# Two-layer hybrid decoder step on one core: where VectorE takes the turned rows in the last four pairs of products

## The chip, the core and the metric

The kernel is one program on one core of one Trainium2 chip. The metric is the device time of one execution in microseconds (us). Before the change the three timed runs took 2153.4, 2157.99 and 2168.16 us, with a median of 2157.99 us. Everything is float32.

## The reference, cut to what matters

One inference step of a two-layer decoder with D_MODEL = 1024 is computed for a prompt of 512 positions and for 8 sample sequences of 8 positions, so for 576 token columns in all. Each layer is a token mixer and a squared-ReLU MLP with 4096 inner columns, each with a residual, and a last RMSNorm gives the output.

```python
def squared_relu_mlp(x, w_up, w_down):
    h = jax.nn.relu(x @ w_up)
    return (h * h) @ w_down

def rmsnorm(x, g):
    y = xf * lax.rsqrt(jnp.mean(xf * xf, axis=-1, keepdims=True) + EPS)
    return (y * g.astype(F32)).astype(x.dtype)

for layer in range(DEPTH):
    ...
    h = h + out
    h = h + squared_relu_mlp(rmsnorm(h, norm_ffn[layer]), w_up[layer], w_down[layer])
return (rmsnorm(h, norm_final), ...)
```

The change lies in the last MLP's down projection, which yields the last `h`, and in the last RMSNorm, which needs each token's sum of squares over all 1024 channels.

## The kernel before, in words

**Layout.** The residual `h` is held with channels on the 128 partitions: 8 blocks of 128 channels (f = 0 to 7) by 576 columns (T). TH = 288 is half of the columns. The output must leave with tokens on the partitions, so each block of `h` is transposed at the end, by TensorE, into rows.

**Pairs.** Every large projection runs in pairs of output blocks by one scheme of seven products instead of eight (Strassen's, in Winograd's form). A pair g has two output blocks n1 and n2 = n1 + 1, and each is made in two column halves. TensorE's side is `seven(g)` (L823 and on). All its matmuls are in the helper `product` (L836): four matmuls of 128x128 by 288 columns each, which the trace shows as eight records. In order the products are P1, P5, P6, P7, P3, P2, P4. They go into four PSUM banks, 0 to 3 for even pairs and 4 to 7 for odd ones. VectorE's side is `pairs`: for the pair that TensorE is at it adds the products up ("mixes" U2 L1676, U4 L1679, C22 L1683, C12 L1686, C21 L1689, and for a down projection `add_first` L1697), and for the next pair it makes four sums of weight blocks (S1 L1622, S2 L1625, S4 L1628, S3 L1630). TensorE waits for weight sums of the pair it works on before P5, P6, P7 and P3, for U2 before P3, and for C22 of the same pair before its last product P4. GpSimd adds C22, C12 and C21 to `h` (L684). ScalarE copies P1 out of PSUM (L1372). Where the next pair belongs to another group of columns of the input, VectorE also makes four sums of activations (T1 L1643, T2 L1649, T3 L1651, T4 L1656) between the mixes.

**The last four pairs.** These are the last four pairs of layer 1's down projection, here n = 0 to 3. Each finishes two channel blocks of `h`: pair n blocks 2n and 2n + 1. In pair n, from n = 1 on, TensorE transposes blocks 2n - 2 and 2n - 1, which pair n - 1 finished, between P6 and P7 (`to_final_rows`, L1295 and L1296). They go into the banks of pair n - 1, which have the same number modulo 2 as those of pair n + 1. So pair n + 1 may not start until these banks are read. That is this wait on TensorE:

```python
if n >= 2:
    pe.wait_ge(sem("rows_taken"), 2 * (n - 1))
seven(g, (lambda: (to_final_rows(2 * n - 2), to_final_rows(2 * n - 1))) if n else None)
```

Blocks 6 and 7 are transposed after the last pair. VectorE takes turned rows in `take_rows(f)`, which waits for `rows_turned` and then has four instructions: a copy of 128x512 (L2162), a copy of 64x128 (L2163), the gain times 128x512 (L2164), and the gain times 64x128 (L2165). The second signals `raw_rows`, for which ScalarE waits with its squares and row sums (L1577), and the fourth signals `rows_taken`. `rows_between(g)` calls it: for n = 0 it only waits for the gain and clears 40 columns of row sums (L2171), and for n = 1 to 3 it takes blocks 2n - 2 and 2n - 1.

**The order.** Each engine's program is written out, and each engine works through its own in order. What VectorE has before it in its program decides how early it gets to a piece of work. After the last pair VectorE takes blocks 6 and 7 and adds the row sums up (L2180), ScalarE takes a root (L1580), VectorE the reciprocal (L2182), both scale the rows (L2186, L1583), and SyncE stores them.

Of the kernel before, what the change touches and what calls it, by code (L numbers as in the profile page):

```python
# [120 lines left out]
PAIRS = [("in", 0, 0, _j, _m) for _j in range(5) for _m in range(2)]  # L121
# [12 lines left out]
def pairs_of(kind, layer):  # L134
    return [g for g in range(NPAIR) if PAIRS[g][:2] == (kind, layer)]


def c11_before(g, kind):
    return sum(GOES[p[0]] == kind for p in PAIRS[:g])


def chunk_of(g):
    return CHUNKS.index(PAIRS[g][:3])
# [81 lines left out]
def hybrid_step(nc, I, O, where0, where1, decay_step):  # L225
    ctx = ExitStack()
    with ctx:
# [5 lines left out]
        def sem(name):  # L233
            if name not in sems:
                sems[name] = ctx.enter_context(nc.semaphore(name))
            return sems[name]
# [162 lines left out]
        def sums_at(g):  # L399
            return (tsum_in, ssum_in, p1_in, u24_in) if PAIRS[g][0] == "in" else (tsum, ssum_w, p1, u24)  # L400
# [1187 lines left out]
        def _(dve):  # L1588
# [25 lines left out]
            def weight_sum(g, name):  # L1614

                (arrived, count), a11, a12, a21, a22 = sums_of(g)
                s1, s2, s4 = (sums_at(g)[1][:, g % 2, a] for a in range(3))
                if name == "S1":
                    dve.wait_ge(arrived, count)
                    if g >= 2:  # L1620
                        dve.wait_ge(sem("product"), 7 * (g - 2) + PROD["P3"])
                    ins = tt(s1, a21, a22, ALU.add)  # L1622
                elif name == "S2":
                    dve.wait_ge(sem("weight_sums"), 4 * g + SUMS["S1"])
                    ins = tt(s2, s1, a11, ALU.subtract)  # L1625
                elif name == "S4":
                    dve.wait_ge(sem("weight_sums"), 4 * g + SUMS["S2"])
                    ins = tt(s4, a12, s2, ALU.subtract)  # L1628
                else:
                    ins = tt(a21, a11, a21, ALU.subtract)  # L1630
                ins.then_inc(sem("weight_sums"), 1)
# [27 lines left out]
            def mix(g, name):  # L1659

                kind, _, c, j, m = PAIRS[g]
                n1 = (j if kind in ("in", "up") else j % 2) * 4 + 2 * m
                _, _, first, u = sums_at(g)
                u2, u4 = u[:, g % 2, 0, :], u[:, g % 2, 1, :]
                bank = [ps[:, 4 * (g % 2) + b, 0:TH] for b in range(4)]
                if kind in ("in", "up"):
                    c22, c12, c21 = big[:, n1 + 1, TH:T], big[:, n1, TH:T], big[:, n1 + 1, 0:TH]
                else:
                    c22, c12, c21 = (xouts[PAIRS[g][:2]][:, g % 2, a, :] for a in range(3))
                    d = c11_before(g, "down")  # L1670
                    if d >= 2 and name[0] == "C":
                        dve.wait_ge(sem("h_added"), 3 * (d - 2) + {"C22": 1, "C12": 2, "C21": 3}[name])
                if name == "U2":
                    dve.wait_ge(sem("p1_copied"), g + 1)
                    dve.wait_ge(sem("product"), 7 * g + PROD["P6"])
                    ins = tt(u2, bank[1], first[:, g % 2, :], ALU.add)  # L1676
                elif name == "U4":
                    dve.wait_ge(sem("mixed"), 5 * g + MIX["U2"])
                    ins = tt(u4, bank[2], u2, ALU.add)  # L1679
                elif name == "C22":  # L1680
                    dve.wait_ge(sem("product"), 7 * g + PROD["P7"])
                    dve.wait_ge(sem("mixed"), 5 * g + MIX["U4"])
                    ins = tt(c22, bank[3], u4, ALU.add)  # L1683
                elif name == "C12":
                    dve.wait_ge(sem("product"), 7 * g + PROD["P3"])
                    ins = tt(c12, bank[1], u4, ALU.add)  # L1686
                else:
                    dve.wait_ge(sem("product"), 7 * g + PROD["P4"])
                    ins = tt(c21, bank[3], u2, ALU.add)  # L1689
                ins.then_inc(sem("mixed"), 1)  # L1690

            def add_first(g):
                _, _, c, j, m = PAIRS[g]
                n1 = j % 2 * 4 + 2 * m
                dve.wait_ge(sem("product"), 7 * g + PROD["P2"])
                hh = h[:, n1, 0:TH]
                tt(hh, ps[:, 4 * (g % 2), 0:TH], hh, ALU.add).then_inc(sem("c11_out_down"), 1)  # L1697

            def first_weight_sums(kind, layer):
                for name in SUMS:  # L1700
                    weight_sum(pairs_of(kind, layer)[0], name)

            def place_queries(n):

                a, f, q = n // 8, n // 4 % 2, n % 4
                at = 64 * a + 32 * f
                cp(q4[32 * q:32 * q + 32].rearrange("p (n a f) t -> p a f n t", a=2, f=2)[:, a, f],
                   big[at:at + 32, EV_Q:EV_Q + HB, SEQ:T])

            def under_in(g):  # L1710

                if g == 0:
                    dve.wait_ge(sem("mixed"), MIX["C21"])
                    for a in range(2):
                        own(cp(es[0][:, a, :, HIST:HIST + NS], big[:, a, SEQ:T].rearrange("p (b s) -> p b s", b=NB)))
                        cp(hcopy[:, a, :].rearrange("p (b t) -> p b t", b=NB), es[0][:, a, :, NS:NS + HIST])
                    cp(hcopy_p, big[:, 0:2, SEQ - HIST:SEQ]).then_inc(sem("ext_ready"), 1)
                if g == 2:
                    dve.wait_ge(sem("lg_in"), 32)
                    for a in range(2):  # L1720
                        ins = nc.vector.reduce_sum(page_sums[:, a, :], lg[:, a].rearrange("p s h -> p h s"), AX.X)
                    ins.then_inc(sem("page_sums_made"), 1)
                if 5 <= g < 9:
                    dve.wait_ge(sem("queries_scaled"), 3)
                    for n in range(4):
                        place_queries(4 * (g - 5) + n)

            def pairs(every, last=None):

                for g in every:  # L1730
                    follow = g + 1 <= every[-1]
                    turn = follow and chunk_of(g + 1) != chunk_of(g)
                    q = chunk_of(g) + 1
                    if follow:
                        weight_sum(g + 1, "S1")
                    mix(g, "U2")
                    if follow:
                        weight_sum(g + 1, "S2")
                    mix(g, "U4")
                    if turn:  # L1740
                        act_sum(q, "T1")
                    if follow:
                        weight_sum(g + 1, "S4")
                    mix(g, "C22")
                    if turn:
                        act_sum(q, "T2")
                        act_sum(q, "T3")
                    if follow:
                        weight_sum(g + 1, "S3")
                    mix(g, "C12")  # L1750
                    if GOES[PAIRS[g][0]] == "down":
                        add_first(g)
                    mix(g, "C21")
                    if turn:
                        act_sum(q, "T4")
                    if last:
                        last(g)

            for f in range(KD):
                s = drained("x", f)  # L1760
# [21 lines left out]
            own(ts(z[0], z[0], 0.0, None, ALU.min))  # L1782
            act_sum(0, "T3")
            act_sum(0, "T4")
            pairs(pairs_of("in", 0), under_in)
            dve.wait_ge(sem("c11_out_in"), c11_before(pairs_of("in", 0)[-1] + 1, "in"))
            nc.vector.memset(rstd[:, :], 0.0).then_inc(sem("gates_zeroed"), 1)
            s = drained("hist_out", 0)
            for a in range(2):
                cp(hout[:, a * P:(a + 1) * P], ps[0:NB * HIST, 2 * s + a, 0:P])  # L1790
                last = cp(hout_p[:, a * P:(a + 1) * P], ps[0:HIST, 2 * s + a, P:2 * P])
# [210 lines left out]
                for name in names:  # L2002
                    act_sum(chunk_of(pairs_of(kind, layer)[0]), name)

            def mlp(layer, last=None):
                first_weight_sums("up", layer)
                norm(2 * layer + 1, PROW["norm_ffn"] + layer * KD, chunk_of(pairs_of("up", layer)[0]))
                all_act_sums("up", layer, ("T2", "T3", "T4"))
                pairs(pairs_of("up", layer) + pairs_of("down", layer), last)

            all_act_sums("out", 0)
            pairs(pairs_of("out", 0))
# [6 lines left out]
            for n in range(R):  # L2019
                dve.wait_ge(sem("gate_exp"), n + 1)  # L2020
                e, g = swish[:, n, :], big[:, OD_RG + n, :]
# [8 lines left out]
            for g in range(4):  # L2030
                last = tt(w8[:, g, :].rearrange("p (b t) -> p b t", b=NB),
                          corner[:, g:g + 1, :].broadcast_to([TS, NB, NS]),
                          cst1("same_s").rearrange("p (b t) -> p b t", b=NB), ALU.mult)
            last.then_inc(out_of["vector"], 1)
            wait_emptied(dve, FIRST["mu"] + 1)
            for f in range(4):
                g = big[:, OD_GV + f, :]
# [18 lines left out]
            for f in range(4):  # L2056
                g = big[:, OD_GV + f, :]
# [162 lines left out]
```

## Time and profile before

| | |
|---|---|
| timed runs | 2153.4, 2157.99, 2168.16 us, median 2157.99 |
| profiled execution, its own time | 2158.41 us |
| its span, first to last instruction | 2156.5 us |
| mean granted TensorE clock | 0.962 |
| TensorE matmuls busy | 1965.2 us, 91% |
| VectorE busy | 1057.2 us, 49% |
| ScalarE busy | 342.2 us, 16% |
| GpSimd busy | 192.1 us, 9% |

The profiled execution is 0.42 us above the median of the runs. It takes 1.91 us more than its span. The chain that ended last is TensorE for 87% of the span. The four pairs that this document is about run from 2070.21 to about 2139 us of the span, and what follows them to the end takes some 17 us.

### The profile page before, as it was taken

The numbers are of one execution on the slowest core, as the hardware profiler recorded it, in microseconds if no ns is written. First come the engines' busy times: TensorE is split into PE (matmuls) and PEld (weight loads), VectorE is DVE, ScalarE is ACT, GpSimd is POOL, SyncE is SP. The second block draws the span as 40 slices with busy tenths as digits, with TensorE's granted clock in tenths as the row PEclk, the third lists the DMA queues.
The fourth block names the chain that finished last, engine by engine and source line by source line (L and its number), as shares of the span: only waits on it lengthen the run. The fifth ranks groups of instructions, "written<-read, shape, count | busy, mean of one in ns | idle before, by whom it ended". The sixth has DMA issues, their size and how long they took to land.

```text
span 2156.5 us, 39410 instructions
## 1 busy us (share of the span) xinstructions
PE 1965.2 (91%) x15991; PEld 1453.2 (67%) x15991; DVE 1057.2 (49%) x1920; ACT 342.2 (16%) x816; POOL 192.1 (9%) x228
## 2 busy tenths in 40 slices
PE   6999788888888669899999998999989899999996
PEld 3776555555555437677777776777767677777774
DVE  4545766776667653533344442324363533344453
ACT  2102122222222111122210001111010122210002
POOL 1400000000000002000012221000001000012220
PEclk9999899999999989999999999999889999999998
DMA  5122999998999991222222222212021222222211
GB/s 172 44 74 91 349 329 359 355 353 313 346 336 361 370 372 51 74 79 79 78 79 78 78 79 79 78 40 81 22 71 40 78 78 78 77 76 76 75 51 44
DMA packets 127600, 320.30 MB, mean 149 GB/s; under 512 B 9852, under 2 KB 10130, under 8 KB 127294
## 3 DMA queue, kind: packets, MB, share of 16 engines
q1 hardware_dynamic: 123874, 304.65, 39.1%
q0 software_dynamic: 3296, 12.98, 1.7%
q8 instruction: 128, 2.10, 0.4%
q14 instruction: 50, 0.41, 0.1%
q10 hardware_dynamic: 252, 0.16, 0.0%
HBM read 309.20 MB, written 8.55 MB: 147 GB/s over the span
## 4 chain that ended last, share of the span: by engine, by line
PE 87%; DVE 5%; issue 4%; DMA 2%; ACT 1%; SPq 1%; ACTq 0%; DVEq 0%
PE ps L836 52%; PE ps L1018 6%; PE ps L1049 4%; PE ps L1149 3%; PE ps L1150 3%; PE ps L983 2%; PE ps L972 2%; PE ps L971 2%; PE ps L751 2%; PE ps L752 1%; PE ps L995 1%; PE ps L780 1%; PE ps L781 1%; PE ps L1026 1%; DMA wring<-in_cache_v 1%
## 5 line engine op out<-in xcount | busy, mean ns | idle before, releaser
L836 PE MATMUL ps<-work 128*128 128x288 f32 x1152 | 297.2, 412 | 11.9 <-DVE work L1649 7.8
L836 PE MATMUL ps<-xn,wring 128*128 128x288 f32 x1008 | 269.3, 411 | 16.7 <-DVE xn L1602 15.7
L836 PEld LDWEIGHTS ps<-work 128*128 128x128 f32 x1152 | 223.0, 194 | 75.0 <-issue 12.8
L836 PE MATMUL ps<-big,wring 128*128 128x288 f32 x944 | 251.8, 411 | 7.6 <-DVE big L2165 7.6
L1839 DVE STREAM_TRANSPOSE work<-work 128x768 f32<-128x768 f32 x256 | 235.3, 955 | 32.3 <-DMA work<-in_cache_k 32.2
L836 PEld LDWEIGHTS ps<-xn,wring 128*128 128x128 f32 x1008 | 193.7, 193 | 71.5 <-issue 16.5
L836 PEld LDWEIGHTS ps<-big,wring 128*128 128x128 f32 x944 | 181.6, 193 | 58.6 <-DVE big L2165 8.5
L1676 DVE TENSOR_TENSOR work<-ps,work 128x288 f32<-128x288 f32 x72 | 32.9, 457 | 320.9 <-PE ps L836 320.9
L1018 PE MATMUL ps<-work,big 32*32 32x256 f32 x6144 | 144.7, 396 | 48.9 <-issue 46.8
L684 POOL TENSOR_TENSOR h<-h,xn 128x288 f32<-128x288 f32 x96 | 106.0, 1107 | 812.6 <-DVE xn L1683 697.5
L1018 PEld LDWEIGHTS ps<-work,big 32*32 32x32 f32 x6144 | 91.6, 104 | 89.2 <-issue 61.9
L836 PE MATMUL ps<-work,wring 128*128 128x288 f32 x544 | 143.1, 407 | 0.0
L1049 PE MATMUL ps<-wring 128*32 128x192 f32 x2048 | 115.3, 364 | 25.3 <-issue 14.1
L1372 ACT ACTIVATE work<-ps 128x288 f32<-128x288 f32 x72 | 29.5, 410 | 625.1 <-PE ps L836 625.1
L836 PE MATMUL ps<-big,work 128*128 128x288 f32 x480 | 124.6, 406 | 0.0
L836 PEld LDWEIGHTS ps<-work,wring 128*128 128x128 f32 x544 | 103.6, 190 | 28.4
L1049 PEld LDWEIGHTS ps<-wring 128*32 128x32 f32 x2048 | 64.7, 120 | 66.7 <-issue 27.2
L836 PEld LDWEIGHTS ps<-big,work 128*128 128x128 f32 x480 | 91.4, 190 | 25.0
L836 PE MATMUL ps<-xn,work 128*128 128x288 f32 x336 | 88.4, 406 | 0.0
L1149 PE MATMUL ps<-xn,wring 128*128 128x288 f32 x256 | 83.2, 407 | 0.0
L1150 PE MATMUL ps<-xn,wring 128*128 128x288 f32 x256 | 83.1, 406 | 0.0
L1438 ACT ACTIVATE wring<-ps,stats 128x1024 f32<-128x1024 f32 x32 | 35.6, 1113 | 256.1 <-DVE stats L1904 256.1
(356 smaller groups left out, 2356.8 us busy)
## 6 DMA issues: line engine op xcount, KB each, us to landing
work<-in_cache_k SPq DMA_DIRECT2D x256, 384.0 KB, 6.7
wring<-in_cache_v SPq DMA_DIRECT2D x256, 384.0 KB, 6.1
wring<-in_w_up SPq DMA_DIRECT2D x16, 2048.0 KB, 9.0
wring<-in_w_down SPq DMA_DIRECT2D x16, 2048.0 KB, 7.8
wring<-in_w_in_odd SPq DMA_DIRECT2D x6, 2048.0 KB, 9.0
wring<-in_w_in_even SPq DMA_DIRECT2D x5, 2048.0 KB, 14.2
wring<-in_w_out_odd SPq DMA_DIRECT2D x2, 2048.0 KB, 7.7
big<-in_x_prompt SPq DMA_DIRECT2D x1, 2048.0 KB, 9.1
```

The source lines that it names most:

```text
L684: pool.tensor_tensor(hs[name], hs[name], xouts[kind, layer][:, g % 2, a, :], ALU.add)\
L751: mm(bankA(s, TH), w, rhs[k][:, 0:TH], start=(k == 0), stop=(k == ks - 1))
L836: last = mm(bank, w[:, k, :], x[:, k, :], start=k == 0 and not onto, stop=k == 3, skip_group_check=onto)
L971: mm(ps[:, 0, 0:w], big[r, EV_Q + hd // 2, i * P:w], big[r, EV_K + hd // 2, 0:w], start=True, stop=False)
L972: mm(ps[:, 0, 0:w], ident[:, hd:hd + 1].broadcast_to([P, P]), gates[:, 0:w], start=False, stop=False)
L983: last = mm(ps[:, 1, j * P:(j + 1) * P], eb[:, n % 2, j * P:(j + 1) * P], diag[:, n % 2, :], start=True, stop=True)
L1018: mm(ps[32 * c:32 * c + 32, 4 + q, 0:256], qcur[r, b % 2, c, n // 2, n % 2, :], group_keys(q, g, 2 * HC * c + n), start=(n == 0), stop=Fal ...
L1049: last = mm(ps[32 * c:32 * c + 32, 3, 0:HC * D], pTs[:, p, 32 * c:32 * c + 32], v_ring[:, n % VSLOTS, HC * D * c:HC * D * (c + 1)], start= ...
L1149: mm(bankA(s, TH), w, xn[:, k, 0:TH], start=(k == 0), stop=(k == KD - 1))
L1150: last = mm(bankB(s, TH), w, xn[:, k, TH:T], start=(k == 0), stop=(k == KD - 1))
L1438: act_f(probs.rearrange("p (g q k) -> p q g k", g=GP, q=4), ps[:, 4:8, 0:256].rearrange("p q (g k) -> p q g k", g=GP), ACT.Exp, bias=shift ...
L1839: nc.vector.transpose(x, x).then_inc(sem("k_turned"), 1)
```

## The change

`rows_between` was called at the end of a pair, behind C21. It is now called in the middle of one, behind U4. Since `pairs` is used for all projections, the calls that go with the input projection (`under_in`) keep their old place at the end of a pair by a line of their own, and no other projection passes anything. No instruction is added or removed, on any engine. Only VectorE's order differs.

```diff
-            def pairs(every, last=None):
+            def pairs(every, between=None):
@@
                     mix(g, "U4")
+                    if between:
+                        between(g)
                     if turn:
                         act_sum(q, "T1")
@@
                     if turn:
                         act_sum(q, "T4")
-                    if last:
-                        last(g)
+                    if PAIRS[g][0] == "in":
+                        under_in(g)
@@
-            pairs(pairs_of("in", 0), under_in)
+            pairs(pairs_of("in", 0))
@@
-            def mlp(layer, last=None):
+            def mlp(layer, between=None):
...
-                pairs(pairs_of("up", layer) + pairs_of("down", layer), last)
+                pairs(pairs_of("up", layer) + pairs_of("down", layer), between)
```

The function passed in is the same as before:

```python
def rows_between(g):
    n = g - pairs_of("down", 1)[-4]
    if n == 0:
        dve.wait_ge(sem("gain_in"), 16)
        own(nc.vector.memset(sumsq, 0.0))
    if n >= 1:
        take_rows(2 * n - 2)
        take_rows(2 * n - 1)

mlp(1, rows_between)
take_rows(KD - 2)
take_rows(KD - 1)
```

VectorE's program before, from U4 of pair n = 1 to the first weight sum that follows it (`work`, `xn`, `h` and `big` are regions of SBUF, `ps` is PSUM, `wring` holds weights, and of the eight instructions that take two blocks the first four stand here):

```order
L1679 TENSOR_TENSOR work<-ps,work 128x288 [waits mixed]
L1628 TENSOR_TENSOR work<-wring,work 128x512 [waits weight_sums]
L1683 TENSOR_TENSOR xn<-ps,work 128x288 [waits mixed,product,h_added]
L1630 TENSOR_TENSOR wring<-wring 128x4x128
L1686 TENSOR_TENSOR xn<-ps,work 128x288 [waits product,h_added]
L1697 TENSOR_TENSOR h<-ps,h 128x288 [waits product]
L1689 TENSOR_TENSOR xn<-ps,work 128x288 [waits product,h_added]
L2162 COPY big<-ps 128x512 [waits rows_turned]
L2163 COPY big<-ps 64x128
L2164 TENSOR_TENSOR big<-ps,work 128x4x128
L2165 TENSOR_TENSOR big<-ps,work 64x128
...
L1622 TENSOR_TENSOR work<-wring 128x512 [waits product,weights_in_0]
```

The same stretch now (L2162 to L2165 are L2164 to L2167 in the changed file):

```order
L1679 TENSOR_TENSOR work<-ps,work 128x288 [waits mixed]
L2164 COPY big<-ps 128x512 [waits rows_turned]
L2165 COPY big<-ps 64x128
L2166 TENSOR_TENSOR big<-ps,work 128x4x128
L2167 TENSOR_TENSOR big<-ps,work 64x128
...
L1628 TENSOR_TENSOR work<-wring,work 128x512 [waits weight_sums]
L1683 TENSOR_TENSOR xn<-ps,work 128x288 [waits mixed,product,h_added]
L1630 TENSOR_TENSOR wring<-wring 128x4x128
L1686 TENSOR_TENSOR xn<-ps,work 128x288 [waits product,h_added]
L1697 TENSOR_TENSOR h<-ps,h 128x288 [waits product]
L1689 TENSOR_TENSOR xn<-ps,work 128x288 [waits product,h_added]
```

The eight instructions that take two blocks have moved ahead of S4 for the next pair and of C22, S3, C12, the first add and C21. The same holds for n = 2, and for n = 3, which has no next pair and so no weight sums. In n = 0 the clearing of the row sums has moved likewise. The rows of TensorE, ScalarE and SyncE are the same as before.

## Rows read from the trace of the kernel before

**Rows 1.** The page, part 1: busy us (share of the span) and instructions.

```profile
PE 1965.2 (91%) x15991; PEld 1453.2 (67%) x15991; DVE 1057.2 (49%) x1920; ACT 342.2 (16%) x816; POOL 192.1 (9%) x228
```

**Rows 2.** Windows of the last pairs: us, busy by engine, then clock, DMA share, GB/s.

```profile
2098.60:2102.40 3.80, 0.03 (x1) 0.00 (x0) 3.67 (x10) 0.00 (x0) 0.79 (x1) 0.92 0.00 0
2102.40:2120.30 17.90, 17.88 (x66) 13.54 (x66) 4.55 (x9) 0.41 (x1) 1.96 (x2) 0.83 0.00 0
2120.30:2124.20 3.90, 0.12 (x1) 0.00 (x0) 3.63 (x9) 0.00 (x0) 0.79 (x1) 1.00 0.00 0
```

**Rows 3.** Timeline of TensorE: start, us, instructions [idle before them and its releaser].

```profile
2083.79 2.10 PE L836 MATMUL ps<-big,wring 128*128 128x288 f32 x8
2090.59 0.27 PE L1296 MATMUL ps<-c,h 128*64 128x128 f32 x1
2096.52 2.10 PE L836 MATMUL ps<-work,wring 128*128 128x288 f32 x8
2102.42 4.21 PE L836 MATMUL ps<-big,wring 128*128 128x288 f32 x8 [3.79 <-DVE big L2165]
2118.31 2.10 PE L836 MATMUL ps<-work,wring 128*128 128x288 f32 x8
2124.20 2.21 PE L836 MATMUL ps<-big,wring 128*128 128x288 f32 x8 [3.79 <-DVE big L2165]
2137.04 2.10 PE L836 MATMUL ps<-work,wring 128*128 128x288 f32 x8
```

**Rows 4.** Timeline of VectorE, pair n = 1 and the start of n = 2.

```profile
2090.85 0.45 DVE L1679 TENSOR_TENSOR work<-ps,work 128x288 f32<-128x288 f32 x1
2091.22 0.68 DVE L1628 TENSOR_TENSOR work<-wring,work 128x512 f32<-128x512 f32 x1
2092.90 0.46 DVE L1683 TENSOR_TENSOR xn<-ps,work 128x288 f32<-128x288 f32 x1 [1.00 <-PE ps L836]
...
2098.73 0.46 DVE L1689 TENSOR_TENSOR xn<-ps,work 128x288 f32<-128x288 f32 x1 [1.55 <-PE ps L836]
2099.11 0.68 DVE L2162 COPY big<-ps 128x512 f32<-128x512 f32 x1
...
2102.29 0.67 DVE L1622 TENSOR_TENSOR work<-wring 128x512 f32<-128x512 f32 x1
```

**Rows 5.** Short windows at the first wait and six us later, columns of Rows 2.

```profile
2101.50:2102.40 0.90, 0.00 (x0) 0.00 (x0) 0.90 (x4) 0.00 (x0) 0.00 (x0) 0.67 0.00 0
2108.40:2109.40 1.00, 1.00 (x5) 0.84 (x4) 0.00 (x0) 0.00 (x0) 0.00 (x0) 0.88 0.00 0
```

**Rows 6.** Timeline of TensorE's weight loads: those of P4 in pair n = 1.

```profile
2096.28 1.89 PEld L836 LDWEIGHTS ps<-work,wring 128*128 128x128 f32 x8
```

**Rows 7.** Timeline of VectorE in an earlier pair that has activation sums, and its window.

```profile
2064.06 1.35 DVE L1643 TENSOR_TENSOR work<-big 128x1152 f32<-128x1152 f32 x1
2065.33 0.69 DVE L1628 TENSOR_TENSOR work<-wring,work 128x512 f32<-128x512 f32 x1
2065.93 0.45 DVE L1683 TENSOR_TENSOR xn<-ps,work 128x288 f32<-128x288 f32 x1
...
2055.00:2070.00 15.00, 15.00 (x64) 11.76 (x63) 8.68 (x12) 0.41 (x1) 3.01 (x2) 1.00 0.00 1
```

**Rows 8.** Behind the last pair: timelines of TensorE and VectorE.

```profile
2140.32 0.27 PE L1296 MATMUL ps<-c,h 128*64 128x128 f32 x1
2141.14 0.27 PE L1296 MATMUL ps<-c,h 128*64 128x128 f32 x1
...
2139.63 0.68 DVE L2162 COPY big<-ps 128x512 f32<-128x512 f32 x1
2144.41 0.66 DVE L2162 COPY big<-ps 128x512 f32<-128x512 f32 x1
```

**Rows 9.** The chain that ended last: start, us, what.

```profile
2145.30 1.58 ACT big L1577 x10
2146.90 0.21 DVE hstat L2180
```

## The prediction

> **What bounds the kernel now.** I read the shares first. TensorE's matmuls fill 91% of the span and VectorE 49% [rows 1]. So work on VectorE matters only where TensorE waits for it. The change touches only the last four pairs, so I cut those into windows [rows 2]. In 2098.60 to 2102.40 and in 2120.30 to 2124.20 TensorE does 0.03 and 0.12 us of work, while VectorE is busy for 3.67 and 3.63. Between them the clock is 0.83 of full speed. The timeline of TensorE tells whom it waits for [rows 3]: the first product of pairs n = 2 and n = 3 comes after 3.79 us of idle time each, both ended by L2165, the last instruction that takes turned rows. VectorE's timeline shows why [rows 4]. Blocks 0 and 1 have been turned since about 2090.59 + 0.27 = 2090.86 [rows 3]. VectorE idles for 1.00 us before C22 and 1.55 before C21, and takes them only from 2099.11 on, behind C21. That is when TensorE has nothing left but the pair that needs their banks. Taking two blocks lasts 2102.29 - 2099.11 = 3.18 us, or 1.59 each [rows 4].
>
> **The change, part by part.**
>
> *Undisturbed pace.* In pair n = 1 P1 starts at 2083.79 and P4 at 2096.52, 12.73 us apart [rows 3]. One product's pace is 1.94 us (P4's end before the second wait, 2118.31 + 1.94 = 2120.25, is where the window of idle time begins [rows 2]): 12.73 is six of them (11.64) and 1.09 for the two blocks turned in between. The 2.10 shown for a product's eight records is a little more, since they overlap with the next ones [rows 3]. So a pair with turning takes 14.67 us when nothing is waited for.
>
> *TensorE's path.* P4 of n = 1 starts at 2096.52 and P4 of n = 3 at 2137.04, which is 40.52 us. Two undisturbed pairs would be 29.34. The excess is **11.18 us**, in four terms. From the end of P4's pace (2098.46) to 2102.42: 3.96. Pair n = 2 from P1 to P4, 2118.31 - 2102.42 = 15.89 against 12.73: 3.16. From 2120.25 to 2124.20: 3.95. Pair n = 3, 12.84 against 12.73: 0.11.
>
> The 3.16 are the clock. It falls in the last 0.90 us of the first wait (0.67 there, a mean of the two levels 2.4 and 1.2 GHz), and is back within 2108.4 to 2109.4 [rows 5]. The eight records that then take 4.21 us take 2.21 behind the second wait [rows 3]. That second wait, just as long, left the clock at 1.00 [rows 2]. So one of two equal gaps cost the clock. If the gaps go, I take the clock term as gone with them, whole. Its bounds are 0 (the fall comes anyway) and, from two falls instead of one in an execution, 6.3.
>
> The Trainium skill, TensorE: Matmul & The Clock Gate, section "What's actually happening", says that an idle window sends the clock to half, that a busy one brings it back, and that the windows run freely, so that the same kernel sees them at another phase each time. By that rule the clock term of an execution before is 0, 3.2 or 6.3 by luck, and the sum below 10.2, 13.4 or 16.5. The trace agrees as far as one gap with a fall and one without can.
>
> *What the takes now do in the middle.* Nothing is added, the eight instructions move. In pair n = 1 U4 starts at 2090.85 and the next instruction at 2091.22 [rows 4]. The turned rows are there (2090.86), so the takes run from 2091.22 to 2094.40. Behind them in VectorE's queue stand S4 of the next pair, C22, S3, C12, the first add and C21. S4 takes 0.60 to the next start (2065.33 to 2065.93, [rows 7]). So C22 starts at 2095.00 and ends at 2095.46, in place of 2092.90. TensorE needs it for P4, whose weight loads start at 2096.28 [rows 6]. That leaves **0.82 us**. S4 and S3 of the next pair are wanted only in that pair. C12 comes at 2095.60 + 0.37 = 2095.97 (S3 0.60), which is still before P2's add and C21, and these stay where they are since P2 and P4 do. GpSimd gets C22 2.1 us later. It adds it in about 0.8 to 1.2 us and has until the next pair's turning, three products into it: 2098.46 + 3 x 1.94 = 2104.3. In n = 2 all is the same, and in n = 3 S4 is missing, so the margin is 0.6 larger. Cost: nothing. An earlier pair bears this out: there T1 pushes S4 and C22 back by 1.27 us, and TensorE is busy for 15.00 of 15.00 us [rows 7]. It was a smaller push than 3.18, so I keep a cost as a rival.
>
> *n = 0.* Clearing the row sums moves in front of S4. It is 0.1 us of an engine that idles, and the gain was there long before. Nothing.
>
> *Behind the last pair.* Before, VectorE takes blocks 4 to 7 in one go from 2139.63 on, and ScalarE's squares follow one block behind. Its last ten start at 2145.30, 0.89 after the copy of block 7 at 2144.41 [rows 8, 9]. Now blocks 4 and 5 are taken in the middle of n = 3. Their squares, and those of blocks 0 to 3, come in the rest of that pair, 6 x 1.57 = 9.4 us [rows 9] of the some 12 between P1's end (2124.20 + 1.94) and P4's (2138.98). What is late next is the turning: block 6 is turned at 2140.32 + 0.27 = 2140.59, so its copy starts at 2140.63 and not at 2139.63, and block 7's at 2142.22 (turned by 2141.41). That is 2144.41 - 2142.22 = **2.19 us** sooner: 3.18 for two blocks, less 0.99 of waiting for the turning. ScalarE's last squares come sooner by as much, and the row sum at 2146.90 and all behind it with them. Bounds: 0, if something else holds the last squares, and 3.18.
>
> *Sum.* 11.18 + 2.19 = 13.4 us. From the profiled execution's 2158.41 that gives 2145.0. That execution is 0.42 above the median of the runs, so from the median it would be 2144.6. I say **2145**.
>
> **The rivals.**
>
> *The clock falls anyway* or at another place: 10.2 us are left, **2148.2**. For: the second gap had no fall, so gap and fall aren't tied one to one. Against: from 2055 to 2070 TensorE never waits and the clock is at 1.00 [rows 7], and the fall begins inside the gap [rows 5]. The rule named above speaks against it too. Chance 0.08.
>
> *C22 becomes the wait.* VectorE works through its queue in order, so anything that makes the takes longer delays C22. Beside the margin of 0.82, takes of twice the length (6.36) would make P4 wait 3.18 - 0.82 = 2.4 us in n = 1 and n = 2 and 1.8 in n = 3, 6.5 in all: 2145.0 + 6.5 = **2151.5**. For: the takes run beside TensorE's writes to PSUM now, while before they ran beside none. Against: the mixes read PSUM in 0.46 us both while TensorE works (C22) and while it stands (C21) [rows 4], and banks differ. Chance 0.06.
>
> *Another wait stands behind the removed one.* TensorE's first product also waits for weights, for the first add, and for mixes of the pair before the last. If one of these comes only by 2102, just the 2.2 of the tail is won: **2156**. Against: 0.13 us lie between the start of S1, behind the takes, and P1 (2102.29, 2102.42), and what else P1 awaits from VectorE belongs to the pair before the last. Chance 0.04. That the change does nothing of what it says is excluded by the order of VectorE's instructions.
>
> *Slower.* The same mechanism at its worst: takes that last 2.5 times as long, 8.0 us, make P4 wait 4.0, 4.0 and 3.4 us, gaps as long as the one that cost the clock. With 3.16 for the clock each time that is 11.4 + 9.5 = 20.9, less the 13.4 won: 7.5 slower, **2166**. It decides where each gap reaches about the 3.8 us that cost the clock, since 3 x (3.8 + 3.2) = 21 is more than 13.4; shorter gaps without a fall would have to sum to 13.4. Nothing in the trace stretches such an instruction. Chance 0.02.
>
> **The numbers.** The forecast has 0.80, the rivals 0.08, 0.06, 0.04 and 0.02. The three timed runs of before lie 4.6 below and 10.2 above their median, more than the change may bring, and what differs in them is in parts that it doesn't touch. A new median may therefore lie some 5 us to either side. For the forecast that gives 2140 to 2150. I reach down to 2138, for the second fall of the clock, and up to 2154, for the clock rival and the first C22 rival with some of that scatter. Faster by over 1% is below 2136.4, 8.6 us under my number. Only a lucky median gives that: 0.05. Slower by over 1% is above 2179.6: 0.02, the slower rival with scatter. Within 1% 0.93, which is about what a measurement of this kernel can tell from no change.
>
> **What would show it.** In the changed kernel's trace TensorE's idle time before the first products of n = 2 and n = 3 should be gone, P1 to P1 14.7 us in all three pairs, and the clock 1.00 to the last product. VectorE's takes should start 0.4 us behind the start of U4, C22 in n = 1 and n = 2 about 4.15 behind it, and the load for P4 should not wait. Behind the last pair the copy of block 6 should wait about 0.6 us for its turning, and the row sum should start 5.7 us behind the end of the last P4's pace, where it was 2146.90 - 2138.98 = 7.9. The forecast is wrong if P4 waits for C22, if another wait takes the place of the 3.79 us, or if the clock falls in the last pairs all the same.

## The result

The changed kernel takes 2147.06 us in the median of ten runs, against 2160.38 for the kernel before in ten runs. The ratio is 0.9934 with a 95% interval of 0.9916 to 0.9951. That is 14.3 us faster, 10.6 to 18.1. The prediction was 2145, with a range of 2138 to 2154, and the change's gain was put at 13.4 us. Most of the weight lay on a change of less than 1%, and less than 1% it is. All ratios here are of fast executions; a slow one in the last timed run, 5795 us at a mean granted clock of 0.35, is left out.

The shares of the changed kernel's page, to be held against [rows 1], say nearly nothing: the same work in 9.5 us less of span.

```profile
PE 1966.8 (92%) x15991; PEld 1452.5 (68%) x15991; DVE 1057.3 (49%) x1920; ACT 342.2 (16%) x816; POOL 192.5 (9%) x228
```

Windows of the changed kernel over its pairs n = 1, 2 and 3, columns as in [rows 2]:

```profile
2087.70:2102.40 14.70, 14.70 (x68) 11.71 (x67) 8.05 (x18) 0.41 (x1) 3.10 (x3) 1.00 0.00 1
2102.40:2117.00 14.60, 14.60 (x67) 11.65 (x66) 8.05 (x18) 0.41 (x1) 3.10 (x3) 1.00 0.00 0
2117.00:2131.70 14.70, 14.70 (x67) 11.50 (x65) 5.83 (x14) 9.16 (x61) 2.38 (x3) 1.00 0.01 1
```

TensorE is busy for the whole of each, and the clock never leaves 1.00. The two windows without TensorE of [rows 2], and the 0.83 of clock between them, are gone.

Timeline of TensorE in the changed kernel, the rows that answer to [rows 3]: P1 of n = 0 to 3, then P4 of n = 3.

```profile
2074.11 2.10 PE L836 MATMUL ps<-big,wring 128*128 128x288 f32 x8
2087.69 2.10 PE L836 MATMUL ps<-big,wring 128*128 128x288 f32 x8
2102.36 2.10 PE L836 MATMUL ps<-big,wring 128*128 128x288 f32 x8
2117.04 2.10 PE L836 MATMUL ps<-big,wring 128*128 128x288 f32 x8
2129.77 2.10 PE L836 MATMUL ps<-work,wring 128*128 128x288 f32 x8
```

P1 to P1 is 13.58 us where no blocks are turned in between (n = 0), and then 14.67 and 14.68. No row shows idle time ahead of it. VectorE's timeline in pair n = 1, to be read beside [rows 4], has U4, the first copy, the last instruction of the takes, S4 and C22:

```profile
2094.75 0.45 DVE L1679 TENSOR_TENSOR work<-ps,work 128x288 f32<-128x288 f32 x1
2095.12 0.68 DVE L2164 COPY big<-ps 128x512 f32<-128x512 f32 x1
...
2098.11 0.27 DVE L2167 TENSOR_TENSOR big<-ps,work 64x128 f32<-64x128 f32 x1
2098.30 0.67 DVE L1628 TENSOR_TENSOR work<-wring,work 128x512 f32<-128x512 f32 x1
2098.90 0.44 DVE L1683 TENSOR_TENSOR xn<-ps,work 128x288 f32<-128x288 f32 x1
```

C22 starts 4.15 us behind U4 and ends at 2099.34. The weight loads of P4, on TensorE's own timeline, come 0.84 us later and wait for nothing:

```profile
2100.18 1.89 PEld L836 LDWEIGHTS ps<-work,wring 128*128 128x128 f32 x8
```

Behind the last pair, VectorE's timeline and then the chain that ended last, for [rows 8, 9]:

```profile
2133.36 0.69 DVE L2164 COPY big<-ps 128x512 f32<-128x512 f32 x1 [0.92 <-PE ps L1296]
2134.96 0.67 DVE L2164 COPY big<-ps 128x512 f32<-128x512 f32 x1
```

```profile
2134.28 1.57 ACT big L1577 x10
2135.87 1.58 ACT big L1577 x10
2137.47 0.21 DVE hstat L2182
```

Only blocks 6 and 7 are left there. The copy of block 6 waits 0.92 us for its turning.

**One measure for all runs.** The executions of one kernel differ by up to 17 us. In its traces what differs lies ahead of these pairs: in the three traces of the kernel before, P1 of n = 2 starts at 2097.63, 2102.42 and 2114.28 us. So I compare the stretch from the start of P1 of n = 0 to the start of the row sum, which holds all that the change moves. It is 2146.90 - 2070.21 = 76.69 us before and 2137.47 - 2074.11 = 63.36 us with the change, 13.33 less. The worked sum was 13.4. The difference of the two spans, 9.5, is these 13.3 less 3.9 by which the changed kernel's trace came later to P1 of n = 0. Each run below is one profiled execution, except where a ratio is given.

### The profile page after: what moved, and what is told of

Read it like the earlier page. It is cut to its first block, busy times and chain, and to the rows that moved or that the text cites. A ratio compares the mean times of both kernels' runs of the same rounds, so it can differ in the third digit from the quotient of the medians.

```text
span 2147.0 us, 39411 instructions
## 1 busy us (share of the span) xinstructions
PE 1966.8 (92%) x15991; PEld 1452.5 (68%) x15991; DVE 1057.3 (49%) x1920; ACT 342.2 (16%) x816; POOL 192.5 (9%) x228
## 4 chain that ended last, share of the span: by engine, by line
PE 88%; issue 4%; DVE 4%; DMA 2%; SPq 1%; ACT 1%; ACTq 0%; DVEq 0%
PE ps L836 52%; PE ps L1018 6%; PE ps L1049 4%; PE ps L1149 3%; PE ps L1150 3%; PE ps L972 2%; PE ps L971 2%; PE ps L983 2%; PE ps L751 2%; PE ps L752 1%; PE ps L995 1%; PE ps L780 1%; PE ps L781 1%; PE ps L1026 1%; DMA work<-in_cache_k 1%
```

## The experiments

### One half at a time

Takes in the middle for n = 1 and 2 alone:

```diff
-                    if between:
+                    if between and g != pairs_of("down", 1)[-1]:
                         between(g)
...
+                    if between and g == pairs_of("down", 1)[-1]:
+                        between(g)
```

> The takes in the middle of n = 1 and n = 2, at the end of n = 3. I measure from the start of P1 of n = 0 to the start of the row sum: 76.69 us before, 63.36 with the change. Theory (two gaps and the clock 11.18 us, tail 2.19): the gaps are gone, the clock stays at 1.00, the tail is as before, 65.5 us. Rival (the tail's gain depends on the gaps, or the takes of n = 1 and 2 in the middle delay P4): more than 66, or 63.4.

The stretch takes 65.53 us. The two gaps were worth 76.69 - 65.53 = 11.16, and what is left over to 63.36 is 2.17 for the tail, the work behind the last pair.

The other half, with the two conditions exchanged:

> The takes at the end of n = 1 and n = 2, in the middle of n = 3. Theory: two gaps of 3.8 us are back, the tail is 2.19 us shorter than before: from P1 of n = 0 to the row sum 74.5 us if the clock falls in one of the gaps, 71.3 if in none, 77.7 if in both. Rival (the clock's fall is tied to the place, not to the gap's phase): 74.5 in every execution, with the fall at the first gap.

The stretch takes 74.54 us, so the tail alone is 2.15. The two halves sum to the whole, 11.16 + 2.15 = 13.31. The clock fell at the first gap and not at the second, as in the first trace of before, so this run doesn't tell the theory from the rival.

### Where in the pair

Behind C12, with the call moved from `mix(g, "U4")` to it:

```diff
                     mix(g, "C12")
+                    if between:
+                        between(g)
```

> The takes behind C12 instead of behind U4, in all three pairs. Theory (any place from which they end before the next pair's P1 is as good): they run from about 11.45 to 14.6 us after the pair's P1, P1 of the next pair would start at 14.67 and waits 0.2 at most: 63.4 to 64.0 us from P1 of n = 0 to the row sum. C22 is back at its old time. Rival (the takes need the middle, since the first add and C21 now queue behind them): P1 of the next pair or the tail late by 1 us or more each.

The stretch takes 63.74 us. This is how the end of the room looks. TensorE's weight loads for the P1 of n = 2, in that run:

```profile
2108.41 1.75 PEld L836 LDWEIGHTS ps<-big,wring 128*128 128x128 f32 x8 [0.37 <-DVE big L2167]
```

They wait 0.37 us, and P1 to P1 grows by 0.19, twice (the start of n = 2 and that of n = 3). So the middle isn't special. What is wanted is a place from which the takes of 3.18 us end before the next P1's weight loads and hold up nothing behind them that TensorE wants sooner.

Behind the first add, one step on:

```diff
                         add_first(g)
+                    if between:
+                        between(g)
```

> The takes behind the first add, one place before C21, in all three pairs. Theory: they end 1.85 us after the undisturbed start of the next P1, so two gaps of about 1.7 us come, and C21 of n = 3 is 1.5 us late for the tail: 63.4 + 3.7 + 1.5 = 68.6 us from P1 of n = 0 to the row sum, with the clock at 1.00, since the gaps are half as long as the one in which it fell. Rival (any gap can cost the clock): 71.8.

The stretch takes 68.99 us, with a clock of 1.00 behind both gaps. The first products of n = 2 and n = 3 on TensorE's timeline:

```profile
2103.53 2.21 PE L836 MATMUL ps<-big,wring 128*128 128x288 f32 x8 [1.78 <-DVE big L2167]
2120.26 2.21 PE L836 MATMUL ps<-big,wring 128*128 128x288 f32 x8 [1.79 <-DVE big L2167]
```

The gaps came about as worked out (68.6 was expected), and the tail lost its 1.5. Two gaps without a fall don't show yet that short ones never have one.

### The margin at P4

The takes of blocks 0 to 5 twice as long:

```diff
+                if f < KD - 2:
+                    at = 3 * T + 1280 * (f % 2)
+                    cp(xnf[:, at:at + 512], ps[:, base, :])
+                    cp(xnf[0:TS, at + 512:at + 640], b)
...
                 cp(raw[:, f, 0:NT, :], a)
```

> The changed kernel with the four instructions that take a block of turned rows issued twice for blocks 0 to 5, the first time into scratch. Theory (margin of 0.82 us between the end of C22 and the weight loads of P4): C22 comes 3.18 us later still, P4 waits 2.4 us in n = 1 and n = 2 and 1.8 in n = 3, so 63.4 + 6.5 = 69.9 us from P1 of n = 0 to the row sum; gaps of this length leave the clock at 1.00. Rival (other slack hides it, as with the activation sums in earlier pairs): under 66.

The stretch takes 69.08 us, with P4 waiting. TensorE's timeline of that run, P4 of n = 1, 2 and 3:

```profile
2088.14 2.21 PE L836 MATMUL ps<-work,wring 128*128 128x288 f32 x8 [2.00 <-DVE xn L1683]
2105.08 2.21 PE L836 MATMUL ps<-work,wring 128*128 128x288 f32 x8 [2.00 <-DVE xn L1683]
2120.94 2.21 PE L836 MATMUL ps<-work,wring 128*128 128x288 f32 x8 [0.92 <-DVE xn L1683]
```

L1683 is C22. From P4 to P4 are 16.94 us in place of 14.67, so the delay is 2.27 where 2.4 was expected, and in n = 3 about 1.2 and not 1.8. I had left out there that S2 is missing too and U4 comes half a microsecond sooner. The rival that other slack hides a late C22 falls: the margin was real, 0.82 by the working and 0.84 in the changed kernel's trace. The takes use most of the room ahead of C22: 3.18 us of some 4.0.

### What a gap costs the clock

The kernel before, with 21 further pauses in which VectorE copies two banks of PSUM to scratch behind C21, each twice, and the next P1 waits:

```diff
+PAUSES = [g for _l in range(2) for _n, g in enumerate(pairs_of("down", _l)) if _n % 4 < 3 and (_l, _n) < (1, 12)]
...
                     mix(g, "C21")
+                    if g in PAUSES:
+                        pause(g)
...
+                if g - 1 in PAUSES:
+                    pe.wait_ge(sem("paused"), PAUSES.index(g - 1) + 1)
```

> The kernel before with 21 further gaps like its two: in 21 earlier down pairs of both layers VectorE copies four banks into scratch behind C21, eight instructions of 3.18 us in all, and the next pair's P1 waits for them. Theory (a gap of 3.8 us costs 3.95 us and, at some phases only, 3.16 for the clock): 83 us for the gaps, and 5 to 18 falls in the 21, 16 to 57 us, so 2257 to 2298 us; the records show some gaps with a fall and some without. Rival A (each such gap costs the clock, and the second one of before was the exception): 21 falls, 2307. Rival B (the fall belongs to the place, not to gaps): no falls in the new gaps, 2241.

2303.5 us, a ratio of 1.0653 (1.0599 to 1.0707) or 141 us. My theory named 5 to 18 falls; there are 21 in 21, nearest to rival A's 2307. The costs are not equal. From the end of one gap to the end of the next it is 20.45 to 20.52 us mostly, against 17.64 without a fall (13.58 + 3.95 + 0.11 for the restart), so 2.8 to 2.9 for the clock. In four it is 19.1 or 19.3, so 1.5 to 1.7. The first products behind two of these four gaps and behind one of the others, on TensorE's timeline:

```profile
2010.76 3.67 PE L841 MATMUL ps<-big,wring 128*128 128x288 f32 x8 [3.79 <-DVE xn L1740]
2029.86 3.31 PE L841 MATMUL ps<-big,wring 128*128 128x288 f32 x8 [3.79 <-DVE xn L1740]
2049.19 4.21 PE L841 MATMUL ps<-big,wring 128*128 128x288 f32 x8 [3.80 <-DVE xn L1740]
```

The length of the first product behind a gap tells at once: 2.21 is no fall, 4.21 is half speed from its start. Summed: 21 x 4.06 = 85, and 17 x 2.85 + 4 x 1.6 = 55, together 140.

With half the pause (`range(1)` in place of `range(2)` for the blocks copied):

> The same 21 places with half the pause, four instructions of 1.59 us. Theory: the next P1 is 2.4 us late each time, 50 us, and gaps this short leave the clock at 1.00: 2208 us. Rival (every gap can cost the clock, in proportion to its length): some 5 falls more, 2224.

2247.1 us, a ratio of 1.0391 (1.0338 to 1.0444) or 84 us, and my theory of no falls (2208) fell. The rival with its 5 falls (2224) was too low as well: of the 21 gaps of 2.2 us, 14 cost the clock. From gap to gap it is 16.05 us without a fall and 17.74 with one, so 1.69 each. Two gaps of that run, equally long, and the four us behind each, as windows:

```profile
1193.30:1195.50 2.20, 0.01 (x1) 0.01 (x1) 2.10 (x6) 0.00 (x0) 0.79 (x1) 1.00 0.23 63
1195.50:1199.50 4.00, 4.00 (x17) 3.16 (x18) 0.54 (x1) 0.41 (x1) 0.00 (x0) 1.00 1.04 401
1209.30:1211.50 2.20, 0.04 (x1) 0.00 (x0) 2.05 (x6) 0.00 (x0) 0.79 (x1) 1.00 0.00 0
1211.50:1215.50 4.00, 3.96 (x10) 2.90 (x11) 0.59 (x1) 0.37 (x1) 0.00 (x0) 0.60 0.00 0
```

Behind the first the clock is 1.00, and behind the second it is 0.60. In the second case it is still at 1.00 through the gap and falls once TensorE works again. The records sum to 21 x 2.47 + 14 x 1.69 = 76 us, inside the interval of 73 to 96.

Two more traces of the unchanged kernel:

> The kernel before, unchanged, for another trace. In the traces so far 21 of 21 added gaps of 3.8 us cost the clock, 1.6 to 3.0 us each, and so did the first of the two gaps of before, but not the second. Theory (the clock term of the two gaps depends on where the fall comes in them, and differs from one execution to the next): 73.5 us for gaps and tail without any clock term, plus 1.6 to 6, so 75 to 79 us from P1 of n = 0 to the row sum, not always 76.7. Rival (the place fixes it): 76.7 again, 3.2 at the first gap and none at the second.

> As the run before it, a third trace of the unchanged kernel, with the same two expectations: another split of the clock term between the two gaps, or 76.7 us with all of it at the first.

The stretch took 76.59 and 76.69 us. The third trace is like the first: 4.21 for the first product of n = 2 and 2.21 for that of n = 3. The second is not:

```profile
2114.28 3.59 PE L836 MATMUL ps<-big,wring 128*128 128x288 f32 x8 [3.79 <-DVE big L2165]
...
2128.50 2.10 PE L836 MATMUL ps<-work,wring 128*128 128x288 f32 x8
...
2134.40 3.77 PE L836 MATMUL ps<-big,wring 128*128 128x288 f32 x8 [3.79 <-DVE big L2165]
...
2148.80 2.10 PE L836 MATMUL ps<-work,wring 128*128 128x288 f32 x8
```

P1 to P4 is 14.22 and 14.40 us, where 12.84 is a restart without a fall, so the clock costs 1.4 and 1.6. So the split changes from execution to execution, as the theory said, and the rival that the place fixes it is out. But the total came out alike, which the theory did not say: 2.9 to 3.1 us in all three traces of the kernel before, and 3.1 with the tail alone moved. It isn't fixed either. In the run with short pauses the same two gaps of 3.8 us cost 1.7 and 1.7, together 3.4, and in the one with long pauses 1.7 and 0.

### Block 6 turned sooner

```diff
                 final_h(pe, f, "down", 1)
-                pe.wait_ge(sem("mixed"), 5 * pair + MIX["C21"])
+                if f == KD - 2:
+                    base = 4 * ((pair - 1) % 2)
+                    pe.wait_ge(sem("rows_taken"), KD - 2)
+                else:
+                    pe.wait_ge(sem("mixed"), 5 * pair + MIX["C21"])
```

`take_rows(KD - 2)` reads from these banks.

> The changed kernel with block 6 turned behind the last P4 without waiting for C21, into the banks of the pair before the last, which the takes in the middle of n = 3 have freed. Theory (what is late next behind the last pair is the turning of block 6): its take starts some 0.8 us sooner, then block 7's turning, which needs GpSimd's last add, sets the end: 62.6 us from P1 of n = 0 to the row sum against 63.4. Rival (block 7 alone sets the end): 63.3. Too little to see in the time.

The stretch takes 62.57 us, 0.79 less than with the change alone. VectorE's copies of blocks 6 and 7 in that run:

```profile
2135.20 0.69 DVE L2168 COPY big<-ps 128x512 f32<-128x512 f32 x1
...
2136.91 0.69 DVE L2168 COPY big<-ps 128x512 f32<-128x512 f32 x1
```

The copy of block 6 follows C21 (started at 2134.72) without a wait. Block 7's comes 1.71 us behind it where 1.59 is the pace, so it is now held by its turning, by 0.1 us. Before that turning TensorE waits for GpSimd's last add:

```profile
2136.10 0.66 PE L1299 MATMUL ps<-c,h 128*128 128x128 f32 x4 [0.94 <-POOL h L684]
```

> The changed kernel with block 6 turned early, as in the run that gave 62.6 us from P1 of n = 0 to the row sum against 63.4, now timed. Theory: 0.8 us less than the change alone, so a ratio to the kernel before of 0.993, not to be told from the change's 0.9934. Rival: the early turning costs elsewhere, ratio over 0.995 and over 63.4 us in the trace.

The ratio to the kernel before is 0.9928 (0.9898 to 0.9959), and the stretch again 62.57 us. It is the shortest stretch of all versions. The timing can't tell it from the change alone.

## Why the prediction was right

**What bounds.** That VectorE's takes behind C21 hold TensorE twice was right: with the takes moved, the gaps are gone, and no other wait took their place. The run with the takes behind the first add brings gaps back in the size worked out from where the takes end, and the two halves add up to the whole.

**The gaps, 11.18.** Measured 11.16 with the tail left as it was. Of it 3.96 + 3.95 are the waits, as read.

**The clock, 3.16 within it.** Right in size for this pair of traces, and wrong in the picture beside it. I had taken from [rows 2] that one of two equal gaps costs the clock, and bounded the term by 0 and 6.3. In 23 added or original gaps of 3.8 us in one run 22 cost the clock, 1.5 to 2.9 us each. What made the term good is that the two gaps, 20 us apart, cost about 3.0 together in all three traces of this kernel, twice as 3.0 and 0 and once as 1.4 and 1.6. The prediction gave no reason for that, and in the two runs with pauses ahead of them the same two gaps cost 1.7 and 3.4, so the close match of this term is in part luck. Why the second gap is spared when the first is hit in full is open: no run here changes only the distance between the two, and in the run with long pauses neighbouring gaps, 20.5 us apart, mostly cost 2.8 to 2.9 us each. The rule of the clock's free-running windows (the Trainium skill, TensorE: Matmul & The Clock Gate, section "What's actually happening") agrees with the trace in that equal gaps of 2.2 us fall on either side. It does not by itself give that sum, nor would it have told that a gap as short as 2.2 us costs the clock, as 14 of 21 did here.

**The rival of the clock that falls anyway** is out: with no gap it stays at 1.00 to the last product, in the changed kernel's trace. First products slowed by the clock (up to 4.21 us for 2.10) stand in these pairs only behind a gap.

**C22.** 4.15 us behind U4, margin 0.84 for 0.82. The rival that the takes run longer beside TensorE's writes is out: 3.18 us there as before. Its price was nearly right too, 69.1 us of the stretch for 69.9.

**The tail, 2.19.** Measured 2.15 to 2.17. The turning of block 6 is late next, by 0.92. The prediction's sign for it, a wait of about 0.6, was too small; its own working had 0.99 from start to start, which fits.

**The slower rival** had takes of 8 us as its condition. Takes of 6.4 us, in the run with doubled takes, still left the kernel faster: 69.08 against 76.69. One bound in it was wrong: I asked for gaps of 3.8 us before the clock pays, and gaps of 2.2 did. None of the three waits in the run with doubled takes, 0.9 to 2.0 us, cost it.

**The total.** 14.3 us by the clock on the wall and 13.3 by the trace agree within the interval of 10.6 to 18.1. That the forecast is 2.1 us under the measured median says little: it stands on three runs of the kernel before with a median of 2157.99, and the ten have 2160.38, from which 13.4 less is 2147.0. The interval of the difference is 7.5 us wide, so a match that close to 2147.06 is luck.

## What to carry to other kernels

Where one engine reads buffers that another must have back, look for the place in its order at which the data are there already and it idles, and count what queues behind the moved work up to its own next deadline: here some 4.0 us of work fitted in front of C22, the first of it that TensorE wants, before TensorE felt it, and the takes need 3.18. A gap of TensorE can cost more than its length: 2.2 us cost 1.1 more on average (14 x 1.69 over 21), and 3.8 us cost 2.6 more (55 over 21), while five gaps and waits of 0.9 to 2.0 us cost nothing more. With executions that scatter by up to 17 us, compare a stretch between two landmarks of the trace; it agreed to 0.1 us in three traces of the kernel before.

## What the runs showed of the hardware

- TensorE working at full clock, then a gap: of 21 repeated gaps of 3.79 us all cost the clock, 1.5 to 1.7 us of loss in four and about 2.7 to 2.9 in the others. Of 21 gaps of 2.20 us 14 did, 1.69 each. Of the two gaps of 1.78 and 1.79 and the three waits of 2.00, 2.00 and 0.92 none did.
- The fall can come after the gap, when TensorE works again: a clock of 1.00 through a 3.79 us gap and 0.72 in the 3 us behind it. The gap before n = 2 in the run with short pauses, and the two windows behind it:

```profile
2183.40:2187.20 3.80, 0.02 (x1) 0.02 (x1) 3.71 (x10) 0.00 (x0) 0.79 (x1) 1.00 0.01 2
2187.20:2190.20 3.00, 3.00 (x9) 2.31 (x10) 0.53 (x1) 0.00 (x0) 0.00 (x0) 0.72 0.00 0
2190.20:2193.20 3.00, 3.00 (x10) 2.17 (x10) 0.00 (x0) 0.41 (x1) 0.00 (x0) 0.71 0.00 0
```

- VectorE's copies out of PSUM (128x512) take 0.67 to 0.68 us in the middle of a pair, while TensorE writes to other banks (changed kernel), and 0.67 to 0.68 us in the two gaps, while it stands still (kernel before).
